# Mixture-of-experts tiles cut at 32 rows: sixteen expert tiles against thirteen shared ones

## The reference

```python
def moe(x, router_w, router_bias, w_gate, w_up, w_down):
    scores = jax.nn.sigmoid(jnp.einsum('btd,de->bte', x, router_w))
    # best of 4 groups, then the top 2 of its 4 experts: two of 16 experts per token, weights in combine
    for e in range(N_EXPERTS):
        h = jax.nn.silu(x @ w_gate[e]) * (x @ w_up[e])
        y = y + (h @ w_down[e]).astype(x.dtype) * combine[..., e:e + 1]
```

## Time and profile before

| | |
|---|---|
| time of one launch, median of 3 | 1356.27 us (1355.74 to 1358.8) |
| the profiled execution: its time | 1357.32 us |
| the profiled execution: its span | 1355.5 us |
| mean granted TensorE clock, share of full speed | 0.955 |
| PE busy | 1217.7 us, 90% of the span |
| DVE, ACT, POOL busy | 607.8, 266.5, 220.0 us |
| moved by DMA | 216.78 MB |
| expert loop, layer 0 (first gate_up to last down) | 483.2 to 673.2 us |
| expert loop, layer 1 | 1113.8 to 1304.0 us |

### The profile page before, as it was taken

The page is one execution under the profiler, slowest core; times in us unless marked ns, Lnnn a source line. Parts: engine busy times, 40 slices in busy tenths (PEclk is TensorE's granted clock), DMA queues, the critical chain, the costliest instruction groups (busy, mean ns, idle before and its releaser), DMA issues.

```text
span 1355.5 us, 13771 instructions
## 1 busy us (share of the span) xinstructions
PE 1217.7 (90%) x4743; PEld 693.4 (51%) x4743; DVE 607.8 (45%) x1432; ACT 266.5 (20%) x630; POOL 220.0 (16%) x385
## 2 busy tenths in 40 slices
PE   8999999999999579999849799999999939999966
PEld 4447777545744244444325455775764424444422
DVE  2178888313723546433355130530443355643316
ACT  1204434122300001111102213332320001111110
POOL 0105445202001120000063200000001111000013
PEclk9999999998999789999969899999999969999978
DMA  8113012325361659999652410000115177999733
GB/s 333 62 63 140 1 68 102 119 90 34 51 217 57 211 171 372 345 368 370 251 187 72 169 62 0 1 0 1 63 42 206 43 241 267 360 362 367 266 140 120
DMA packets 108452, 216.78 MB, mean 160 GB/s; under 512 B 5053, under 2 KB 72157, under 8 KB 107233
## 3 DMA queue, kind: packets, MB, share of 16 engines
q1 hardware_dynamic: 90544, 153.35, 32.0%
q0 software_dynamic: 17552, 61.76, 14.5%
q10 hardware_dynamic: 288, 0.80, 0.2%
HBM read 181.02 MB, written 34.85 MB: 159 GB/s over the span
## 4 chain that ended last, share of the span: by engine, by line
PE 81%; DVE 9%; issue 3%; DMA 3%; ACT 2%; POOL 1%; SPq 0%; DVEq 0%; POOLq 0%; ACTq 0%
PE pair L1374 16%; PE pair L1283 10%; PE pair L1020 10%; PE pair L1393 8%; PE pair L1031 5%; PE pair L1203 5%; PE pair L1137 4%; PE pair L1467 3%; PE pair L1240 3%; PE pair L1516 2%; PE pair L1362 2%; PE pair L1238 1%; PE pair L1497 1%; PE pair L1061 1%; PE pair L1221 1%
## 5 line engine op out<-in xcount | busy, mean ns | idle before, releaser
L1020 PE MATMUL pair<-ring,xT 128*128 128x512 f32 (+1 forms) x320 | 138.9, 593 | 0.7 <-DMA ring<-in_even_w_in 0.7
L1374 PE MATMUL pair<-ring,arena 128*128 128x512 f32 x256 | 117.1, 612 | 3.5 <-DVE arena L2173 3.5
L1374 PE MATMUL pair<-arena 128*128 128x512 f32 x256 | 112.5, 592 | 0.0
L1020 PEld LDWEIGHTS pair<-ring,xT 128*128 128x128 f32 (+1 forms) x320 | 57.7, 182 | 76.4 <-issue 75.1
L1137 PE MATMUL pair<-xT,ring 128*128 128x296 f32 x320 | 83.4, 415 | 6.1 <-ACT arena L1552 3.0
L806 POOL TENSOR_SCALAR small<-small 128x1 f32<-128x1 f32 (+3 forms) x45 | 15.8, 352 | 433.7 <-DVE small L2054 390.4
L1374 PEld LDWEIGHTS pair<-ring,arena 128*128 128x128 f32 x256 | 50.0, 197 | 66.5 <-issue 66.5
L2193 DVE COPY arena<-pair 128x256 f32<-128x256 f32 x32 | 13.6, 423 | 156.2 <-PE pair L1382 156.2
L828 POOL TENSOR_TENSOR arena<-arena 128x128 f32<-128x128 f32 x140 | 56.6, 437 | 156.9 <-PE pair L1063 86.4
L1203 PE MATMUL pair<-arena 128*128 128x264 f32 (+5 forms) x280 | 79.1, 412 | 2.2 <-issue 1.4
L1374 PEld LDWEIGHTS pair<-arena 128*128 128x128 f32 x256 | 48.6, 190 | 61.2 <-issue 61.2
(11 more groups left out here) (354 smaller groups left out, 1879.2 us busy)
## 6 DMA issues: line engine op xcount, KB each, us to landing
arena<-in_moe_w_gate SPq DMA_DIRECT2D x16, 1024.0 KB, 7.2
arena<-in_moe_w_up SPq DMA_DIRECT2D x16, 1024.0 KB, 9.8
arena<-in_moe_w_down SPq DMA_DIRECT2D x16, 1024.0 KB, 11.5
ring<-in_moe_w_gate SPq DMA_DIRECT2D x16, 1024.0 KB, 7.9
ring<-in_moe_w_up SPq DMA_DIRECT2D x16, 1024.0 KB, 10.2
ring<-in_moe_w_down SPq DMA_DIRECT2D x16, 1024.0 KB, 12.2
y_rows<-arena SPq DMA_DIRECT2D x32, 512.0 KB, 9.7
ring<-in_even_w_in SPq DMA_DIRECT2D x5, 2048.0 KB, 7.4
```

The source lines that it names most:

```text
L1020: last = pe.matmul(ps[0:P, 0:n], xT[:, k, 128 * i:128 * i + P], w[:, k, :], start=(k == 0), stop=(k == chunks - 1))
L1374: last = pe.matmul(bank, xgT[:, e % 2, k, :], gu[:, k, :], start=(k == 0), stop=(k == KD - 1))
```

## The change

The sixteen experts no longer own 128 slots each. Their regions have 96, 96, 128 and 96 slots, four times over (`CAPS`), and stand end to end, 1664 slots in 52 blocks of 32: 13 tiles (`NX`) instead of 16. A tile holds blocks of one, two (or the end of one and the start of the next) experts: `BLOCKS[x]` names the expert of each of its four blocks, `LAST[e]` the last tile that uses expert e. These come out as

```diff
+CAPS = [96, 96, 128, 96] * 4
+BASE = [sum(CAPS[:e]) for e in range(NE)]
+NX = sum(CAPS) // 128
+NOV = 12
+NSLOTS = (NX + NOV) * 128
+BLOCKS = [[next(e for e in range(NE) if BASE[e] <= 128 * x + 32 * j < BASE[e] + CAPS[e]) for j in range(4)]
+          for x in range(NX)]
+LAST = [max(x for x in range(NX) if e in BLOCKS[x]) for e in range(NE)]
...
-    parts["base"] = np.broadcast_to(128.0 * np.arange(16), (128, 16))
+    parts["base"] = np.broadcast_to(np.array(BASE, np.float32), (128, 16))
+    parts["caps"] = np.broadcast_to(np.array(CAPS, np.float32), (128, 16))
...
-        IX_GROUPS = [range(e, e + 2) for e in range(0, NE, 2)]
+        IX_GROUPS = [range(x, min(x + 2, NX)) for x in range(0, NX, 2)]
...
-        we_in = [signal(f"expert_weights_loaded{b}", [le for le in ALLE if le[1] % 4 == b], 48)
+        ALLX = [(l, x) for l in range(2) for x in range(NX)]
...
+            def load_gate_up(l, e):
+                sp.dma_start(expert_place(e)[0], gu_d[l * NE + e]).then_inc(we_in[e % 4].sem, 16)
+
+            def load_down(l, e):
+                sp.dma_start(expert_place(e)[1], down_d[l * NE + e]).then_inc(we_in[e % 4].sem, 16)
+
             def load_expert(l, e):
-                gu, dn = expert_place(e)
-                s = we_in[e % 4].sem
-                sp.dma_start(gu[:, :, 0:DE], gate_d[l * NE + e]).then_inc(s, 16)
-                sp.dma_start(gu[:, :, DE:2 * DE], up_d[l * NE + e]).then_inc(s, 16)
-                sp.dma_start(dn, down_d[l * NE + e]).then_inc(s, 16)
+                load_gate_up(l, e)
+                load_down(l, e)
...
+                for x in range(NX):
+                    freed = [e + 4 for e in range(NE - 4) if LAST[e] == x]
+                    sp.wait_ge(*gu_ps[(l, x)])
+                    for e in freed:
+                        load_gate_up(l, e)
+                    sp.wait_ge(*dn_ps[(l, x)])
+                    for e in freed:
+                        load_down(l, e)
+                    sp.wait_ge(*y_sa[(l, x)])
+                    sp.wait_ge(*y_sd[(l, x)])
+                    sp.dma_start(y_rows[l][128 * x:128 * x + 128, :], yb[:, x % 2, :]).then_inc(y_st[x % 2].sem, 16)
+                    if l == 0 and x == LAST[12]:
+                        load_item(n_items0)
+                    if l == 0 and x == LAST[13]:
+                        for n in range(n_items0 + 1, n_items0 + 4):
...
-                        pool.dma_start(y_all[128 * (NE + n):128 * (NE + n) + 128, :], zrow).then_inc(zero_st.sem, 16)
+                        pool.dma_start(y_all[128 * (NX + n):128 * (NX + n) + 128, :], zrow).then_inc(zero_st.sem, 16)
...
-                pe.wait_ge(*we_in[e % 4][(l, e)])
+                for x in sorted(set(BLOCKS[e])):
+                    pe.wait_ge(*we_in[x % 4][(l, x)])
                 pe.wait_ge(*xgT_sa[(l, e)])
                 pe.wait_ge(*xgT_sd[(l, e)])
                 if e >= 2:
                     pe.wait_ge(*h_sb[(l, e - 2)])
-                gu, _ = expert_place(e)
                 bank = psum[1][:, 512 * (e % 2):512 * (e % 2) + 512]
                 for k in range(KD):
-                    last = pe.matmul(bank, xgT[:, e % 2, k, :], gu[:, k, :], start=(k == 0), stop=(k == KD - 1))
+                    for j, x in enumerate(BLOCKS[e]):
+                        c = slice(32 * j, 32 * j + 32)
+                        last = pe.matmul(bank[c, :], xgT[:, e % 2, k, c], expert_place(x)[0][:, k, :],
+                                         start=(k == 0), stop=(k == KD - 1))
                 last.then_inc(gu_ps.sem, 1)
...
-                _, dn = expert_place(e)
                 for half in range(2):
                     for k in range(2):
-                        last = pe.matmul(psum[2][:, 512 * half:512 * half + 512], hT[:, e % 2, 128 * k:128 * k + 128],
-                                         dn[:, k, 512 * half:512 * half + 512], start=(k == 0), stop=(k == 1))
+                        for j, x in enumerate(BLOCKS[e]):
+                            c = 32 * j
+                            last = pe.matmul(psum[2][c:c + 32, 512 * half:512 * half + 512],
+                                             hT[:, e % 2, 128 * k + c:128 * k + c + 32],
+                                             expert_place(x)[1][:, k, 512 * half:512 * half + 512],
+                                             start=(k == 0), stop=(k == 1))
...
-                chain(ts(ovn, cnt, 128.0, None, ALU.is_gt))
-                for m in (256.0, 384.0, 512.0):
+                chain(tt(cnt, cnt, const("caps"), ALU.subtract))
+                chain(ts(ovn, cnt, 0.0, None, ALU.is_gt))
+                for m in (128.0, 256.0, 384.0):
                     chain(stt(ovn, cnt, m, ovn, ALU.is_gt, ALU.add))
                 chain(dve.tensor_tensor_scan(ovend, const("ones")[:, 0:NE], ovn, 0.0, ALU.mult, ALU.add))
                 copy(ovi[:, 0:1], ovend[:, NE - 1:NE])
                 chain(tt(cnt, ovend, ovn, ALU.subtract))
-                chain(ts(cnt, cnt, 128.0, float(NE * 128 - 128), ALU.mult, ALU.add))
+                chain(ts(cnt, cnt, 128.0, float(NX * 128), ALU.mult, ALU.add))
+                chain(tt(cnt, cnt, const("caps"), ALU.subtract))
                 chain(tt(ovn, const("base"), cnt, ALU.subtract))
-                chain(ts(R[6], R[5], 128.0, None, ALU.is_lt))
+                chain(tt(R[6], R[5], over_i(const("caps")), ALU.is_lt))
...
-                for e in IX_GROUPS[g]:
+                for x in IX_GROUPS[g]:
                     for i in range(NT):
-                        last = ts(oneh[:, e % 2, i, :], iotab[:, :], 1.0, rk1[:, i, e:e + 1], ALU.add, ALU.is_equal)
+                        for e in sorted(set(BLOCKS[x])):
+                            lo = 32 * BLOCKS[x].index(e)
+                            hi = lo + 32 * BLOCKS[x].count(e)
+                            last = ts(oneh[:, x % 2, i, lo:hi], iotab[:, lo:hi], float(128 * x - BASE[e] + 1),
+                                      rk1[:, i, e:e + 1], ALU.add, ALU.is_equal)
                     last.then_inc(oh_sb.sem, 1)
...
+    tiles_of = lambda w: np.asarray(w).reshape(2 * NE, -1, 128, w.shape[3]).transpose(0, 2, 1, 3)
+    inputs = {**inputs, "moe_w_down": tiles_of(inputs["moe_w_down"]),
+              "moe_w_gate_up": tiles_of(np.concatenate([inputs["moe_w_gate"], inputs["moe_w_up"]], 3))}
```

More of the change, by code:

```diff
@@ L561, in build_step @@
         rt_sb = signal("router_done", [0, 1])
-        oh_sb = signal("onehots_written", [(l, e) for l in range(2) for e in range(NE)])
+        oh_sb = signal("onehots_written", [(l, x) for l in range(2) for x in range(NX)])
         ix_sb = signal("slot_tokens_written", [(l, g) for l in range(2) for g in range(len(IX_GROUPS))])
@@ L578, in build_step @@
         ALLE = [(l, e) for l in range(2) for e in range(NE)]
[L579 removed]
+        ALLX = [(l, x) for l in range(2) for x in range(NX)]
+        we_in = [signal(f"expert_weights_loaded{b}", [le for le in ALLE if le[1] % 4 == b], 32)
                  for b in range(4)]
[L581 to L593 removed]
+        xg_in = [signal(f"expert_rows_loaded{b}", [le for le in ALLX if le[1] % 2 == b], 16) for b in range(2)]
+        xgT_ps = signal("expert_rows_transposed", ALLX)
+        xgT_sa = signal("expert_rowsT_written_act", ALLX)
+        xgT_sd = signal("expert_rowsT_written_dve", ALLX)
+        gu_ps = signal("gate_up_in_psum", ALLX)
+        eg_sb = signal("gate_exp_ready", ALLX)
+        h_sb = signal("hidden_written", ALLX)
+        hT_ps = signal("hidden_transposed", ALLX)
+        hT_sb = signal("hiddenT_written", ALLX)
+        dn_ps = signal("down_in_psum", ALLX)
+        y_sa = signal("expert_out_written_act", ALLX)
+        y_sd = signal("expert_out_written_dve", ALLX)
+        y_st = [signal(f"expert_out_stored{b}", [le for le in ALLX if le[1] % 2 == b], 16) for b in range(2)]
         yg_in = [signal(f"token_rows_gathered{i}", [0, 1], 32) for i in range(NT)]
@@ L752, in _ @@
                 load_expert(l, 1)
-                for e in range(NE):
-                    if e + 4 < NE:
-                        sp.wait_ge(*dn_ps[(l, e)])
-                        load_expert(l, e + 4)
-                    sp.wait_ge(*y_sa[(l, e)])
-                    sp.wait_ge(*y_sd[(l, e)])
-                    sp.dma_start(y_rows[l][128 * e:128 * e + 128, :], yb[:, e % 2, :]).then_inc(y_st[e % 2].sem, 16)
-                    if l == 0 and e == 13:
-                        for n in range(n_items0, n_items0 + 4):
+                for x in range(NX):
[13 more added lines that the diff above has]
+                        for n in range(n_items0 + 1, n_items0 + 4):
                             load_item(n)
@@ L940, in experts @@
                     pool.wait_ge(*x_st[b][last])
-                for e in range(NE):
+                for e in range(NX):
                     for g in range(len(IX_GROUPS)):
@@ L966, in experts @@
                 pool.wait_ge(*zero_st["all"])
-                for b in range(2):
```

(19 more changed lines are left out.)

39 lines of the change are left out of this document (10 added, 29 removed).

## The result

| | before | after |
|---|---|---|
| time of one launch, median of 5 | 1357.06 us (1355.74 to 1360.4) | 1371.32 us (1365.8 to 1371.55) |
| ratio, with its 95% interval | | 1.008 (1.0059 to 1.01) |
| profiled execution: time, span | 1357.32, 1355.5 us | 1371.40, 1369.6 us |
| mean granted TensorE clock | 0.955 | 0.928 |
| PE busy | 1217.7 us | 1171.9 us |

A forecast was written before the change was run, and what follows sets the result against it. PE was taken to bound the expert loop, with DMA close behind. Terms -68.9 + 9.1 + 1.8 + 2.8 + 1.4 + 3.8 = -50.0 took 1357.3 to 1307.3, stated as 1307 us, range 1295 to 1331.

The forecast's parts named there:

- Weights: Expert loop: weight loads nearly keep up, with tight places at experts 6 and 12; +1.4 us for both layers.
- Three tiles: Expert loop: three fewer tiles per layer, each costing PE the same in four column groups as in one piece; -68.9 us.
- Switching: PE changing between full-width transposes and column groups, 0.35 us for each of 26 tiles; +9.1 us.
- One-hots ahead of the loop: DVE's two-piece one-hots for group 0 delay the first gather while PE and POOL wait; +1.8 us for both layers.
- Slot chain: Step 3 of the loop: DVE, already late, comes 1.4 us later with no cover; +2.8 us for both layers.
- Tail of layer 0: Next-stage weights mi1, uk, uv go ahead of the last store, which lands 8.9 us after its data; +3.8 us.
- At nothing: Items priced at zero: three more zeroing transfers on POOL covered by an existing wait, and no overflow tile running.
- Instruction supply: Rival 1: PE's sequencer cannot feed four times as many records in gate/up and down; +96, 1403 us; chance 0.06.
- DMA bound at 360 GB/s: Rival 2: packed weights in the loop run no faster than old ones, PE waits 16.4 us in all; 1322 us; chance 0.2.
- Overflow: Rival 4: an expert beyond 96 rows brings a serial tile of some 25 us; 1332 us for one; chance 0.02.
- wrong if the waits for weights pass 5 us per layer: Sign in the new trace: the forecast fails if PE's waits for expert weights exceed this per layer.
- Its other test: Sign in the new trace: the forecast fails if a tile's gate/up and down lines take over 10.6 us.

The follow-up runs named there:

- e13: Changed kernel with separate gate/up and down counts, gate/up issued earlier, POOL's norm/residual loads behind its last gather, slot chain in step 5, mi1/uk/uv behind combine's first gather: 1301.32 us.
- e15_sixteen_tiles: e13 with 128 slots for every expert again, so sixteen tiles per layer: 1366.14 us.
- e2: Changed kernel with 128 slots per expert again: sixteen one-expert tiles, still in column groups with packed weights: 1366.19 us.
- e3: Kernel before the change with only packed weights, two transfers per expert instead of three: 1357.99 us.
- e14_loads_last_only: e13 without its two small moves: slot chain back in step 3, mi1, uk and uv back ahead of the last store: 1313.61 us.
- e18: e13 with mi1, uk and uv back ahead of the last store; the slot chain stays in step 5: 1302.66 us.
- e6: e5 with mi1, uk and uv issued behind the last store of layer 0 instead of ahead of it: 1336.61 us.
- e12: e5 with POOL's norm/residual loads ahead of tile 11's gather, slot chain in step 5, and mi1, uk, uv behind the combine's first gather: 1334.12 us.
- e8_twelve: e6 with 96 slots for every expert: twelve tiles, and one overflow tile in layer 1: 1358.14 us.
- e17_split_loads_last: e14_loads_last_only with the changed kernel's SP order, so without the earlier issue of gate/up: 1339.76 us.
- e5: Changed kernel with separate gate/up and down counts, SP issuing gate/up once its place is free and both loads ahead of the wait for output copies: 1334.16 us.
- e9: e5 with POOL's norm and residual loads moved from ahead of tile 3's gather to ahead of tile 11's: 1345.71 us.
- e11: Changed kernel with separate gate/up and down counts, its own SP order, and POOL's norm/residual loads moved to tile 11's gather: 1363.52 us.

## Why the prediction was wrong

**The step that failed is "Weights", +1.4 us; it measured 54.2 us of waits and 11.7 us of slower matmuls behind them, 65.9.** It followed the gate/up matrices of experts 6 and 12 to their landing, with bytes and a rate, and never asked for what count PE waits. The transfer that gates tile 4 is expert 6's down matrix, issued as PE asks for it; no bandwidth helps. Expert 7, at tile 5, was missed. The transfers it did follow came out later than it said, too: the gate/up matrix of expert 6 landed at 535.63, 1.6 us after PE had ended the down ahead (534.04), that of expert 12 at 615.27, 3.8 us after (611.46), where 0.7 was forecast. In the kernel before, the down of expert e - 4 ended two whole steps ahead of the gate/up of expert e, always, so the shared count never showed.

Below that, the same step gave SP's order and POOL's 3.5 MB no place of their own, only bytes in a sum over the whole loop. The sum itself was right: 38.6 MB are there in time (in e13 no gate/up waits for them). But a loop that fills the queues is held by the order in each of them.

*Three tiles, -68.9.* Right. Between e15_sixteen_tiles and e13_loads_last the two loops differ by 70.1 us (352.7 to 282.5, first to last gate/up) and the medians by 64.8; 3.1 us of the gap are the longer end (last section). The argument from the router's 16 records held: four groups share each pass, 64 records in 6.87 us like 16 wide ones.

*Switching, +9.1.* 8.2 us in 32 tiles by e2 and e3, 0.26 each instead of 0.35, 6.7 for 26: steps of 11.68 against 11.40.

*One-hots ahead of the loop, +1.8.* PE waited 13.5 us for them against 8.1, but for the gather behind them 4.1 against 7.2: 2.3 net. A group of 20 takes 3.0 us against 1.72 for ten.

*Slot chain, +2.8.* Too small. In e14_loads_last_only, where nothing hides it, the two steps around tile 3 take 28.5 and 28.3 us against 23.8 for two others: 4.7 and 4.5 us, of which 2.96 and 2.75 are PE's wait. Before, it was 1.6 and 1.4, so it grew by 6.3. Moving the chain to step 5 gave 11 us (e14 to e18). In the changed kernel itself it lay under the wait of tile 4, as the prediction said of a later wait there.

*Tail of layer 0, +3.8.* The last store took 9.90 us (8.9 forecast), and from the last gate/up to the next stage's transposes are 43.9 us against 39.0: +4.9. That it can be won back, as e6 and e12 expected, was wrong: with the three loads behind it in either way the gather or PE waits for them (e6; e13 against e18, 1.3 us).

*At nothing.* Unforeseen: 3.1 us at the very end (last section).

One reading was loose: the loop before had more idle places than the one step that was named. Rows 2 show 0.88 us ahead of the first gate/up and 0.52 and 0.90 ahead of the last two downs. They did not move the sum.

With the transfers in time the forecast would have come close: e14, which is the change with its transfers in time, took 1313.6 where the sum without its weights term gives 1305.9. The loops there are 57.6 us shorter than before (57.0 by the sum); the difference is in the tail, the end and between the loops.

**The rivals.** *Instruction supply* (the one on the slower side) is out: with 64 records in 6.87 us, every distance as wide as before plus switching. The result was slower for a reason that was no rival. *DMA bound at 360 GB/s* named two of the three tiles (4 and 9) and the wrong cause: the loop of e13 moves 395 to 420 GB/s over 35 us windows. The Trainium skill's figure of about 358 GB/s per core (DMA: Bandwidth & Descriptors, Specifications) is half of what a stack gives its two cores; with one core at work, as here, it was no bound. *Overflow* was priced at 25 us and costs 43.6 (e8_twelve). The prediction's own test, "wrong if the waits for weights pass 5 us per layer", fired: 27 per layer. Its other test held: the two product lines of an undisturbed tile take 6.87 + 3.57 = 10.4 us, not over 10.6.

## What to carry to other kernels

When a change makes a buffer free later, or its first use come sooner, read for each use which semaphore it waits for, to what count, and which transfer supplies the last increment, before any bandwidth is summed. A loop at a DMA share of 1.00 is held by the order within each queue: put what is needed last behind everything that is needed sooner, and expect that moving it elsewhere ahead of a gather only moves the wait. Waits hide each other: two of the three remedies here gave nothing alone and 23 us together.

## What was not expected of the hardware

- Idling costs twice. Behind waits of 7 to 12.7 us a gate/up took 8.4 to 9.7 us instead of 7.05 (timeline), with a granted clock of 0.58 in the idle window 612 to 623 and first passes 0.85 us apart instead of 0.43. A shorter wait was not cheaper: behind 4.21 us at tile 9 of e17_split_loads_last the gate/up took 9.57. Behind 1.79 us, at its tile 4, it took 7.07.
- A gather behind 3.5 MB of its own queue took 26 to 36 us once SP's gate/ups went out early or the loads stood at tile 11 (e5 to e9, e11, e12), against 10.8 us in the kernel before and medians of 5 to 12 us over a loop's gathers. In the one window looked at, of e12_all, that queue had 28.7% of the DMA engines' time and SP's 65.9%.
- The program's end. From POOL's last issue to the end of the span are 6.4 us in the kernel before, e2, e3 and e15, and 9.4 to 9.5 in the changed kernel and all others. No row shows what fills it. The first four have sixteen tiles and nine overflow regions, the others twelve regions and thirteen tiles, or twelve in e8_twelve, which has 9.4 all the same: the step goes with the regions, not with the tiles. How it does was not tried.
